# Fetching modulation weights in wider units, ahead of parameter loads that move to GpSimd's queue

## The reference, cut to what matters

```
for i in range(2):
    mod = silu(c) @ w_ada[i] + b_ada[i]          # (9, 1024) @ (1024, 6144)
    sh1, sc1, g1, sh2, sc2, g2 = split(mod, 6)
    h = rmsnorm(x, norm_g[i, 0]) * (1 + sc1) + sh1
    ...
```

## Time and profile before

| | us |
|---|---|
| median of 3 runs | 4622.24 |
| lowest and highest of them | 4620.67, 4624.16 |
| the profiled execution, its own time | 4615.82 |
| its span (first to last instruction) | 4614.2 |
| end of the modulation stage in it (layer 1's rows stored) | 189.1 |
| first product of the first head | 230.6 |

### The profile page before, as it was taken

The page is one execution under the profiler, slowest core; times in us unless marked ns, Lnnn a source line. Parts: engine busy times, 40 slices in busy tenths (PEclk is TensorE's granted clock), DMA queues, the critical chain, the costliest instruction groups (busy, mean ns, idle before and its releaser), DMA issues.

```text
span 4614.2 us, 31645 instructions
## 1 busy us (share of the span) xinstructions
PE 3645.7 (79%) x9682; PEld 1472.7 (32%) x9682; DVE 2422.8 (53%) x5830; ACT 683.9 (15%) x1661; POOL 2038.1 (44%) x2169
## 2 busy tenths in 40 slices
PE   5699999997777778777778748779677777877777
PEld 1233333334422223222223335335222232232223
DVE  3223142333876667777751256125866677777630
ACT  1201101011111111111111121010111111111111
POOL 0000101000577767777774100002677767777753
PEclk9799999998899999999999865789899999999999
DMA  9721313122899999999999250225999999999996
GB/s 310 265 95 64 120 48 114 50 91 78 316 409 410 409 409 399 400 406 391 409 409 373 106 76 13 101 65 183 370 409 409 409 397 406 405 404 392 409 390 244
DMA packets 413675, 1287.86 MB, mean 279 GB/s; under 512 B 59636, under 2 KB 83348, under 8 KB 412509
## 3 DMA queue, kind: packets, MB, share of 16 engines
q0 software_dynamic: 309312, 1126.31, 62.5%
q1 hardware_dynamic: 95716, 157.07, 10.7%
q10 hardware_dynamic: 8500, 2.70, 0.3%
HBM read 1257.15 MB, written 28.79 MB: 279 GB/s over the span
## 4 chain that ended last, share of the span: by engine, by line
PE 38%; DMA 21%; POOL 18%; DVE 12%; issue 8%; ACT 1%; SPq 1%; ACTq 0%; DVEq 0%; POOLq 0%
DMA arena<-in_peer_v_dram,arena 10%; POOL arena L1142 9%; PE ps L1450 9%; DMA w<-in_peer_u_dram,arena 9%; POOL w L1142 9%; PE ps L1612 8%; PE ps L1548 3%; DVE arena L1962 3%; PE ps L678 3%; PE ps L1590 3%; DVE w L1962 2%; PE ps L591 2%; PE ps L659 1%; DMA w<-in_w_ada_dram 1%; PE ps L1469 1%
## 5 line engine op out<-in xcount | busy, mean ns | idle before, releaser
L1612 PE MATMUL ps<-arena 128*128 128x512 f32 x4096 | 1998.1, 620 | 621.0 <-DMA arena<-in_peer_v_dram,arena 533.2
L1962 DVE CUSTOM_DVE_ANT_0 w<-w,ps 128x1024 f32<-128x1024 f32 x896 | 1090.2, 1218 | 694.8 <-DMA w<-in_peer_u_dram,arena 694.3
L1612 PEld LDWEIGHTS ps<-arena 128*128 128x128 f32 x4096 | 722.4, 192 | 1872.0 <-DMA arena<-in_peer_v_dram,arena 1167.8
L1142 POOL DMA_INDIRECT arena<-in_peer_v_dram,arena x1040 | 988.3, 950 | 472.2 <-PE ps L1612 238.2
L1142 POOL DMA_INDIRECT w<-in_peer_u_dram,arena x912 | 862.0, 945 | 280.3 <-issue 247.4
L1330 ACT ACTIVATE arena<-ident,arena 128x128 f32<-128x128 f32 x1024 | 393.8, 398 | 1601.3 <-PE ps L1612 1576.6
L1450 PE MATMUL ps<-w,hT 128*128 128x512 f32 (+1 forms) x960 | 422.7, 596 | 3.5 <-DVE arena L1794 3.0
L1086 POOL TENSOR_TENSOR rstd<-var,mhalf 128x5 f32<-128x5 f32 x5 | 5.9, 1186 | 827.1 <-DVE var L1656 827.1
L1104 POOL DMA_DIRECT2D out_dram<-arena x32 | 23.3, 728 | 604.5 <-DVE arena L1747 458.3
L1590 PE MATMUL ps<-hT,w 128*128 128x512 f32 x512 | 275.5, 630 | 0.0
L1450 PEld LDWEIGHTS ps<-w,hT 128*128 128x128 f32 (+1 forms) x960 | 159.6, 170 | 265.7 <-issue 265.7
(11 more groups left out here) (283 smaller groups left out, 2911.1 us busy)
## 6 DMA issues: line engine op xcount, KB each, us to landing
w<-in_w_ada_dram SPq DMA_DIRECT2D x48, 1024.0 KB, 7.5
w<-in_ret_w_in_dram SPq DMA_DIRECT2D x24, 1024.0 KB, 7.2
out_dram<-arena POOLq DMA_DIRECT2D x36, 512.0 KB, 3.3
arena<-in_peer_v_dram,arena POOLq DMA_INDIRECT x1040, 11.2
arena<-in_state_ret_dram POOLq DMA_DIRECT2D x32, 512.0 KB, 4.9
w<-in_peer_w_q_dram SPq DMA_DIRECT2D x16, 1024.0 KB, 7.2
w<-in_peer_u_dram,arena POOLq DMA_INDIRECT x912, 11.9
w<-in_ret_w_out_dram SPq DMA_DIRECT2D x8, 1024.0 KB, 6.0
```

Source lines behind the costliest of these rows:

```text
L1142: pool.indirect_dma_start(ring[:, slot, :], None, table, bass.IndirectOffsetOnAxis(ap=index, axis=0)).then_inc(landed_sem[slot], 16)
L1612: mm = pe.matmul(ps[:, bank + half, :], diag[:, n % DIAGS], v_ring[:, n % RING, half * BW:(half + 1) * BW], start=(n % NE == 0), stop=(n % ...
L1962: dve.tensor_tensor_reduce(row, row, h_ps, 1.0, 0.0, ALU.mult, ALU.add, acts[:, j % 2, s:s + 1]).then_inc(u_used, 1)
```

## The change

The modulation weights come in units: unit n holds half of the rows (row blocks 0 to 3 for even n, 4 to 7 for odd n) of a group of 1024 columns, again 2 MB in two DMAs, and now with 4 KB in each contiguous piece. Two units make a group, which is two of the old blocks. An even unit starts the sums of both blocks in PSUM banks 1 and 2, the odd unit finishes them. So both banks fill at once, and before the next even unit TensorE waits until ScalarE has emptied both. ScalarE's order becomes, for each group: both finished rows of the group before, then the two banks of this group. The two first units are issued right behind the conditioning vectors, ahead of `parameter_loads`; `more_parameter_loads` goes to GpSimd's queue, where it stands behind the wait for the constants.

```diff
-            parameter_loads(sp)
+            def ada_unit(n):
+                wm, col, c0 = w_ada[n // (ADA_BLOCKS // LAYERS)], n % (ADA_BLOCKS // LAYERS) // 2 * 2 * BW, n % 2 * 4
+                dst = w[:, n % 2, :].rearrange("p (c n) -> p c n", c=4)
+                src = wm.rearrange("(c p) n -> p c n", p=P)
+                return [(dst[:, c:c + 2], src[:, c0 + c:c0 + c + 2, col:col + 2 * BW]) for c in (0, 2)]
             sp.dma_start(cond[0:NS, :], c_sample).then_inc(c_ld, 16)
             sp.dma_start(cond[NS:NC, :], c_prompt).then_inc(c_ld, 16)
             for b in range(2):
-                load_block(b, columns(b, w_ada[0], b * BW))
+                load_block(b, ada_unit(b))
+            parameter_loads(sp)
             sp.dma_start(bias, b_ada.rearrange("l (a n) -> a (l n)", a=1).to_broadcast([NC, LAYERS * 6 * D]))\
               .then_inc(tab_ld, 16)
-            more_parameter_loads(sp)
             sp.dma_start(x[:, 0:TP, :], x_prompt[0].rearrange("(t p) n -> p t n", p=P)).then_inc(x_ld, 16)
...
             for n in range(2, ADA_BLOCKS):
                 sp.wait_ge(w_used, n - 1)
-                load_block(n % 2, columns(n % 2, w_ada[n // per_layer], n % per_layer * BW))
+                load_block(n % 2, ada_unit(n))
...
             pool.wait_ge(consts, 4)
+            more_parameter_loads(pool)
...
             def modulation_parts(n):                       # ScalarE
-                act.wait_ge(w_used, n + 1)
+                act.wait_ge(w_used, n // 2 * 2 + 2)
...
             def modulations(first, end):                   # ScalarE
-                for n in range(first, end):
-                    modulation_parts(n)
-                    if n:
-                        modulation_rows(n - 1)
+                for g in range(first, end):
+                    if g:
+                        modulation_rows(2 * g - 2)
+                        modulation_rows(2 * g - 1)
+                    modulation_parts(2 * g)
+                    modulation_parts(2 * g + 1)
...
-            modulations(0, 3)
+            modulations(0, 2)
             sines(act)
-            modulations(3, 5)
+            modulations(2, 3)
             c_transposed(act)
-            modulations(5, 13)
+            modulations(3, 8)
             modulations_out(0)
-            modulations(13, ADA_BLOCKS)
+            modulations(8, ADA_BLOCKS // 2)
+            modulation_rows(ADA_BLOCKS - 2)
             modulation_rows(ADA_BLOCKS - 1)
...
             def modulation_parts(n):                       # TensorE
                 pe.wait_ge(w_ld[n % 2], 32 * (n // 2 + 1))
-                if n >= 2:
-                    pe.wait_ge(part_done, n - 1)
-                for c in range(KC):
-                    j = c % 4
-                    mm = pe.matmul(ps[32 * j:32 * j + 32, 1 + n % 2, :], condT[:, c, :], block_rows(n % 2)[:, c, :],
-                                   start=(c < 4), stop=(c >= 4))
+                if n >= 2 and n % 2 == 0:
+                    pe.wait_ge(part_done, n)
+                rows = w[:, n % 2, :].rearrange("p (c n) -> p c n", c=4)
+                for half in range(2):
+                    for j in range(4):
+                        mm = pe.matmul(ps[32 * j:32 * j + 32, 1 + half, :], condT[:, n % 2 * 4 + j, :],
+                                       rows[:, j, half * BW:(half + 1) * BW], start=(n % 2 == 0), stop=(n % 2 == 1))
                 mm.then_inc(w_used, 1)
...
             def modulations(first, end):                   # TensorE
                 for n in range(first, end):
                     modulation_parts(n)
-                    if n:
-                        modulation_rows(n - 1)
+                    if n >= 2:
+                        modulation_rows(n - 2)
-            modulations(0, 3)
+            modulations(0, 4)
             c_transposes(pe)
-            modulations(3, 9)
+            modulations(4, 9)
...
             modulations(23, ADA_BLOCKS)
+            modulation_rows(ADA_BLOCKS - 2)
             modulation_rows(ADA_BLOCKS - 1)
```

More of the change, by code:

```diff
@@ L992, in _ @@
             for b in range(2):
-                load_block(b, columns(b, w_ada[0], b * BW))
+                load_block(b, ada_unit(b))
+            parameter_loads(sp)
             sp.dma_start(bias, b_ada.rearrange("l (a n) -> a (l n)", a=1).to_broadcast([NC, LAYERS * 6 * D]))\
               .then_inc(tab_ld, 16)
-            more_parameter_loads(sp)
             sp.dma_start(x[:, 0:TP, :], x_prompt[0].rearrange("(t p) n -> p t n", p=P)).then_inc(x_ld, 16)
             sp.dma_start(x[0:NS, TP, :], x_sample[:, 0, :]).then_inc(x_ld, 16)
-            per_layer = ADA_BLOCKS // LAYERS
             for n in range(2, ADA_BLOCKS):
                 sp.wait_ge(w_used, n - 1)
-                load_block(n % 2, columns(n % 2, w_ada[n // per_layer], n % per_layer * BW))
+                load_block(n % 2, ada_unit(n))
             def head_blocks(head, last):
```

## The result

The changed kernel is slower: 4639.19 us in the median of 7 runs (4632.37 to 4641.26), beside 4624.16 (4615.41 to 4629.75) for the kernel before. The ratio is 1.0029, with a 95% interval of 1.0018 to 1.0041. The prediction was 4621 us with a range of 4608 to 4634. The slowdown is small, 15.0 us between the medians, but its interval does not reach 1.

The account below looks back on a forecast made before the run. The weight stream was taken to bound the modulation stage from 48.5 to 119.5 us, TensorE from there to 189.1. Terms -1.4, -7, 0, -2 and +9 sum to -1.4 on 4622.2: about 4621 us, range 4608 to 4634.

Parts of the forecast that it names:

- three tiny loads behind four others: SP's queue at the start: three issues leave the way, so the weight stream begins 1.4 us earlier.
- eight transfers to GpSimd's queue: Start of the stage: of 13.5 us with small pieces, gaps are filled but bytes still paid (6.7 us): about -7.
- GpSimd's price: GpSimd's issue of small-piece loads: 2.9 to 7.4 ns a piece, c done by 14 to 32 us; taken as 0.
- middle stretch: 4 KB pieces and the wait: 48.5 to 119.5 us, 12 units: faster stream against six waits of 1.5 us; 69 us, -2, between -5 and +6.
- last stretch: four waits and the end: 119.5 to 189.1 us, TensorE without cover: waits +6 and end +3, together +9, between +4.5 and +13.
- a clock that leaves 0.81 by much: Sign that the forecast is wrong: the clock's share in the stretch from 119.5 to 189.1 us moves far from 0.81.
- The end behind the last unit: From the last unit to the store of rows: 8.2 us where the old order had 5.2, so +3.
- the forecast's 13.5 us: Start of the stage, 22 to 36 us: the gain if small pieces lie beside the stream at no cost.
- The first rival: Start of the stage: small pieces cost as much as before, unit 2 used at 46 us; +7.6, 4630 us; chance 0.24.
- TensorE's floor of 66.1 us: 48.5 to 119.5 us: six waits of 1.5 us on 57.05 us of work make TensorE the lower bound.
- The second (head hidden wholly, 4611): Start of the stage: small pieces pass while the bias blocks, units come at 421 GB/s; -11, 4611 us; chance 0.27.
- The late GpSimd: Before unit 4: above 11 ns a piece TensorE waits for c; at 15 ns about 4645 us; chance 0.08.

Follow-up runs that it names:

- the repeated run: The changed kernel unaltered, run once more beside other kernels on one chip: 4636.41 us, 1.0035 of the kernel before.
- the run with filled waits: Changed kernel plus four unread products into an unused bank ahead of the wait, before each even unit from 10 on: 4626.47 us, 1.0009 of the kernel before.
- the run with 2 KB: Changed kernel with each unit fetched as two DMAs of 512 columns, pieces of 2 KB: 4637.18 us, 1.0036 of the kernel before.

## Why the prediction was wrong

The stage was read rightly: what it loses is handed on nearly one to one (21.7 us in the stage, 19.4 at the end of the same execution), and the loss fell where TensorE was said to have no room. Term by term, between the two profiled runs:

| term, as the prediction put it | predicted | measured |
|---|---|---|
| three tiny loads behind four others | -1.4 | -1.3 (first unit issued at 1.75 us for 3.05) |
| eight transfers to GpSimd's queue | -7 | -1.6 (the rest of the head's 2.9) |
| GpSimd's price | 0 | 0 |
| middle stretch: 4 KB pieces and the wait | -2 | +2.5 (+0.4 in the repeated run) |
| last stretch: four waits and the end | +9 | +22.2 (+20.6 in the repeated run) |

**The step that failed is the last stretch's +9.** Its mechanism was right in place and count, and nearly in length (1.7 us for 1.5): idle time and the moved row give 6.2 + 2.2 = 8.4. But the wait was priced at itself only. The low clock stood in the sum as a bound, for the rows at the end, and in the middle stretch; that gaps among products at 0.81 of the clock could bring down the clock of all the work around them was put at nothing where TensorE sets the pace, without a reason, and no rival priced it. It measured some 14 us in the profiled run and 9.7 in the repeated one, more than the wait itself (6.2 and 8.7 us of idle time), and the run with filled waits confirms it in the program's time (9 to 12 us). The forecast had named the sign, a clock that leaves 0.81 by much; it went to 0.69 and 0.73. The end behind the last unit, +3 in the forecast, became 10.85 - 5.2 = +5.7, since the last rows ran mostly at the low clock, as in the upper bound (1.86 and 1.82 us for a row's two products).

A section of the Trainium skill bears on this, TensorE: Matmul & The Clock Gate, A second HAM failure mode: psum-queue depth-cycling. It tells of a bf16 kernel in which short idle times between groups of products, from the cycling of its PSUM banks, let the clock swing between its two levels. The traces here agree in kind: 1.7 us gaps of that origin, and the median partial product at 1060 ns for 661.

**The second step that failed is the -7 for the small pieces.** The share of 1.06 at 157 GB/s was read as engines with gaps inside, and gaps there were hardly any. Queued elsewhere the pieces cost the stream nearly as much, now beside units 0 and 1 (share 1.04 at 209 to 298 GB/s): of the forecast's 13.5 us, 10.6 came back as a later unit 1. The first rival's price, nothing beyond the 1.4, was right to 1.6 us, and its 46 us for unit 2 as well (45.6). The rule on which it leaned (the Trainium skill, DMA: Bandwidth & Descriptors, Issuing engines are not separate DMA queues) is borne out by the queue order alone at 0.9997. What does shorten the head is moving less or moving it later: the bias on one partition (6.3 us in the head's window) and x behind unit 17 (5.9 us).

**The middle.** Its -2 rested on two readings that both fell. Pieces of 4 KB bring nothing that the run with 2 KB can tell. And TensorE's floor of 66.1 us, six waits on top of its work, doesn't hold, because five of the six waits come at no cost: four lie inside waits for the stream that are there anyway, one behind the transposes of c. It came out inside its bounds of -5 to +6.

**Rivals.** The second (head hidden wholly, 4611) fell with the head. The late GpSimd fell too: all its loads are issued by 11 us, and TensorE never waits for c nor VectorE for b. Its price per piece was bounded at 2.9 to 7.4 ns; it is 0.4 to 1.0 ns. The three tiny loads came later than forecast: they landed 23 to 26 us after their issue, the last of them some 27 us later than before and not 13, and VectorE waited 23.0 us for it. It cost nothing, as forecast: VectorE's wait for the sines fell from 37.7 to 16.9 us, and it still stands there.

Open is the scatter. The kernel before varies by some 15 us between runs, and its profiled run lay 8.3 us below the median of the 7; a difference of a few us between single windows therefore tells nothing. Why one run of a kernel gets more of its units at the low clock than another was not settled; the size of the clock's part, 9 to 14 us, is as uncertain as that.

## What to carry to other kernels

Where a change makes the units of a stream larger at the same number of PSUM banks, look for the new wait for all banks at once; put independent work into it, or have the banks emptied first. Do not price a gap on TensorE, in a stretch that TensorE bounds, at its length alone: here 6 to 9 us of idle time brought 10 to 14 us more through the clock, where the granted clock was 0.81 before. Moving transfers to another queue gave 2.9 us here, 1.3 of it issue time, with the DMA share at 0.98 before; look instead for transfers that are larger than what is read, or needed late.

## What was not expected of the hardware

Four products that nobody reads, put into the wait before each even unit from 10 on, made the changed kernel 9 to 12 us faster. GpSimd issues a load of 1024 pieces in about 0.95 us and one of 4096 pieces in 1.7 to 1.9 us, so 0.4 to 1.0 ns a piece. A load of 432 KB to 9 partitions held up what stood behind it in its queue: with 48 KB to one partition in its place, unit 2 was used 6.3 us earlier.
